# Two gate tiles moved beside the rotation, the other gates and the latent turns put in one sequence, the combination placed earlier

## What is computed

```python
qkv_a = proj[..., :IN_A]
q_c = proj[..., IN_A:IN_A + B_Q_RANK]
kv_c = proj[..., IN_A + B_Q_RANK:IN_A + B_Q_RANK + B_KV_RANK]
gates = jax.nn.sigmoid(proj[..., IN_A + IN_B:] + b_gate)
g_a, g_b = gates[..., :D_MODEL], gates[..., D_MODEL:]
o_a = mixer_dilated(qkv_a, pos) @ w_o_a
o_b = mixer_mla(q_c, kv_c, k_pe, pos, mla_q_norm, mla_w_uq, mla_kv_norm, mla_w_ukv) @ w_o_b
mix = (g_a * o_a + g_b * o_b) @ w_out
```

## Time and profile before

| | us |
|---|---|
| median of three runs (lowest, highest) | 1642.92 (1642.27, 1648.21) |
| the profiled execution, its own time | 1641.97 |
| its span, first to last instruction | 1640.2 |
| TensorE busy | 1531.1 |
| first rotation and turns | 170.2 to 184.7 |
| first attention, its first score to its last instruction | 185.4 to 340.2 |
| stage with the combination, TensorE's first product to VectorE's last instruction | 340.5 to 378.1 |

### The profile page before, as it was taken

The page is one execution under the profiler, slowest core; times in us unless marked ns, Lnnn a source line. Parts: engine busy times, 40 slices in busy tenths (PEclk is TensorE's granted clock), DMA queues, the critical chain, the costliest instruction groups (busy, mean ns, idle before and its releaser), DMA issues. The chain is left out here.

```text
span 1640.2 us, 18642 instructions
## 1 busy us (share of the span) xinstructions
PE 1531.1 (93%) x7560; PEld 1241.9 (76%) x7560; DVE 809.4 (49%) x1166; ACT 575.8 (35%) x902; POOL 282.6 (17%) x296
## 2 busy tenths in 40 slices
PE   7989699787999999999998999988799999999997
PEld 5878588685677888888886766766678888888885
DVE  4232433357756545434346786377755444324425
ACT  4221533435744433223235322285324222112212
POOL 0000000000032599000003265413222000000000
PEclk9999899789999999999999989989689999999998
DMA  4322121130022323322232212110012233222322
GB/s 174 103 78 80 52 78 46 45 104 26 2 85 93 105 92 103 103 90 90 103 128 62 77 53 77 58 52 27 1 52 77 78 103 103 102 80 100 103 90 77
DMA packets 38858, 129.25 MB, mean 79 GB/s; under 512 B 4676, under 2 KB 23004, under 8 KB 27380
## 3 DMA queue, kind: packets, MB, share of 16 engines
q1 hardware_dynamic: 38484, 127.93, 22.7%
q10 hardware_dynamic: 288, 0.12, 0.0%
HBM read 124.82 MB, written 3.17 MB: 78 GB/s over the span
## 5 line engine op out<-in xcount | busy, mean ns | idle before, releaser
L223 DVE TENSOR_TENSOR ring_lo<-ring_raw,ring_hi 128x2048 fp32r<-128x2048 f32 (+3 forms) x115 | 265.8, 2314 | 203.5 <-ACT ring_hi L213 203.4
L242 PE MATMUL bank<-xT_hi,ring_hi 128*128 128x512 f32 (+3 forms) x920 | 356.2, 387 | 5.9 <-DVE xT_lo L1570 4.7
L242 PE MATMUL bank<-xT_lo,ring_hi 128*128 128x512 f32 (+3 forms) x920 | 352.7, 383 | 0.0
L242 PE MATMUL bank<-xT_hi,ring_lo 128*128 128x512 f32 (+3 forms) x920 | 352.5, 383 | 0.0
L213 ACT CAST ring_hi<-ring_raw 128x2048 fp32r<-128x2048 f32 (+3 forms) x115 | 212.8, 1852 | 241.9 <-DMA ring_raw<-in_w_ff 131.1
L242 PEld LDWEIGHTS bank<-xT_hi,ring_hi 128*128 128x128 f32 (+2 forms) x920 | 174.1, 189 | 47.4 <-issue 7.6
L242 PEld LDWEIGHTS bank<-xT_hi,ring_lo 128*128 128x128 f32 (+2 forms) x920 | 174.0, 189 | 34.3
L242 PEld LDWEIGHTS bank<-xT_lo,ring_hi 128*128 128x128 f32 (+2 forms) x920 | 174.2, 189 | 33.1
L242 PE MATMUL bank<-ring_hi,hid_hi 128*128 128x512 f32 x432 | 169.6, 393 | 3.8 <-DVE ring_lo L223 3.8
L242 PE MATMUL bank<-ring_hi,hid_lo 128*128 128x512 f32 x432 | 169.1, 391 | 0.0
L242 PE MATMUL bank<-ring_lo,hid_hi 128*128 128x512 f32 x432 | 169.0, 391 | 0.0
(11 more groups left out here) (496 smaller groups left out, 2157.8 us busy)
## 6 DMA issues: line engine op xcount, KB each, us to landing
ring_raw<-in_w_ff SPq DMA_DIRECT2D x30, 1024.0 KB, 4.9
ring_raw<-in_w_up SPq DMA_DIRECT2D x22, 1024.0 KB, 4.9
ring_raw<-in_w_proj SPq DMA_DIRECT2D x8, 1024.0 KB, 5.2
ring_raw<-in_w_gates SPq DMA_DIRECT2D x8, 1024.0 KB, 4.9
ring_raw<-in_w_fm SPq DMA_DIRECT2D x12, 512.0 KB, 4.7
ring_raw<-in_w_dn_a SPq DMA_DIRECT2D x6, 1024.0 KB, 4.8
ring_raw<-in_w_proj SPq DMA_DIRECT2D x8, 512.0 KB, 4.5
ring_raw<-in_w_out SPq DMA_DIRECT2D x4, 1024.0 KB, 4.9
```

What stands on the lines that cost most here:

```text
L223: k.nc.vector.tensor_tensor(k.ring.lo[:, g % SLOTS, 0:n], k.raw[:, g % SLOTS, 0:n], plain(k.ring.hi[:, g % SLOTS, 0:n]), ALU.subtract).the ...
L242: mm = k.nc.tensor.matmul(out, x, y, start=first and n == 0, stop=last and n == 3 * len(pairs) - 1)
```

## The change

- `GatesAndTurns` no longer spreads halves evenly. It is given one sequence of tiles (`order`) that share the banks 6 and 7 by their place in it: gates 0 to 12, turn 0, gate 13, turn 1, gate 14, turn 2, gate 15, turns 3, 4, 5. A tile waits until the one two places ahead is released: a gate when kept, a turn when its low part is made.
- Gates 0 and 1 are made at the head of TensorE's stream in the first turn stage, ahead of its wait for the rotation. ScalarE keeps gate 0 between the squares and the scaling of the latents, gate 1 behind the scaling. SP issues chunk 16 there, behind its wait for gate 1.
- The rounds are written out: gates 2 to 12 (22 halves) over rounds 0 to 19, then turns and gates 13 to 15 mixed in rounds 20 to 24, turns 4 and 5 in round 26, behind the last mixes.
- At round 0 ScalarE and VectorE split chunk 15, which gate 1's end no longer asks for.
- In the combination the weights move from tile 7 to 5, exponential from 8 to 6, sums and first addition from 9 to 6, the other additions from 10 and 11 to 7 and 8, the rotation of the queries from 13 to 10.

```diff
-class GatesAndTurns(Beside):
+class GatesAndTurns:
...
+        self.place = {x: n for n, x in enumerate(order)}
+
+    def bank(self, x):
+        return self.k.pb[6 + self.place[x] % 2]
+
+    def released(self, x):
+        kind, n = x
+        return (self.free.sem, self.free.base + n + 1) if kind == "gate" else (self.low.sem, self.low.base + n + 1)
...
+    def sync_begun(self, sp):
+
+        issue_chunks(self.k, sp, self.first + 1 + SLOTS)
...
+    def unit(self, pe, kind, n, half):
+        k, x = self.k, (kind, n)
+        if half == 0 and self.place[x] >= 2:
+
+            pe.wait_ge(*self.released(self.order[self.place[x] - 2]))
+        if kind == "turn":
...
+        g, _, _, pairs, _, _ = self.steps[n]
+        wait_chunk(k, pe, g)
+        w = len(pairs) // 2
+        mm = products(k, self.bank(x)[:, :], pairs[half * w:half * w + w], half == 0, half == 1)
+        if half:
+            mm.then_inc(self.done.sem, 1)
...
+    def act(self, act, r):
         k = self.k
...
+        if r == 0:
+            split_hi(k, act, self.first + 1 + LEAD)
+        for kind, n, half in self.rounds.get(r - 1, ()):
+            if kind == "turn":
+                _, f, dst, gain = self.turns[n]
+                act.wait_ge(self.turned.sem, self.turned.base + n + 1)
+                k.nc.scalar.mul(dst.hi[:, f, :], self.bank((kind, n))[:, :], gain).then_inc(self.high.sem, 1)
+            elif half:
+                self.keep_gate(act, n)
+                if n % 2:
+                    split_hi(k, act, min(self.steps[n][0] + 1 + LEAD, self.end + LEAD))
...
@@ -908,6 +949,8 @@
                 if i < nb:
                     turn(i)
                     turn(i + 1)
+            for r in range(nb + 2, beside.steps_on_pe) if paired else ():
+                beside.pe(pe, r)
...
-            if paired and beside.steps_on_pe > nb:
-                beside.act(act, nb + 1)
+            for r in range(nb + 1, beside.steps_on_pe + 1) if paired else ():
+                beside.act(act, r)
...
             if norms is not None:
-                norms.act(act)
+                norms.squares(act)
+                gates.keep_gate(act, 0)
+                norms.scale(act)
+                gates.keep_gate(act, 1)
...
         @block.tensor
         def _(pe):
+            for n in range(2) if gates is not None else ():
+                for half in range(2):
+                    gates.unit(pe, "gate", n, half)
             if before is not None:
...
+    order = [("gate", n) for n in range(13)] + [("turn", 0), ("gate", 13), ("turn", 1), ("gate", 14), ("turn", 2),
+                                                ("gate", 15), ("turn", 3), ("turn", 4), ("turn", 5)]
+    units = [("gate", n, half) for n in range(2, 13) for half in range(2)]
+    rounds = {r: units[len(units) * r // 20:len(units) * (r + 1) // 20] for r in range(20)}
+    rounds.update({20: [("turn", 0, 0), ("gate", 13, 0)], 21: [("gate", 13, 1), ("turn", 1, 0)],
+                   22: [("gate", 14, 0), ("gate", 14, 1)], 23: [("turn", 2, 0), ("gate", 15, 0)],
+                   24: [("gate", 15, 1), ("turn", 3, 0)], 26: [("turn", 4, 0), ("turn", 5, 0)]})
+    beside = GatesAndTurns(k, steps, evac_gates, turns, order, rounds)
     norms = LatentNorms(k, qc, kvc, 195)
-    stage_turn(k, items, rope_a, norms=norms)
+    stage_turn(k, items, rope_a, sync=beside.sync_begun, norms=norms, gates=beside)
...
     def act(self, act, j):
-        if j == 8:
+        if j == 6:
...
-        elif j == 7:
+        elif j == 5:
             self.weights(dve)
-        elif j == 9:
+        elif j == 6:
             self.sums(dve)
             self.add(dve, 0)
-        elif j in (10, 11):
-            self.add(dve, j - 9)
-        elif j == 13:
+        elif j in (7, 8):
+            self.add(dve, j - 6)
+        elif j == 10:
             self.rope_query(dve)
```

More of the change, by code:

```diff
@@ L727, in __init__, with squares @@
         self.sq, self.mean, self.root, self.scaled = (k.sig("norm_" + n) for n in ("sumsq", "mean", "root", "scaled"))
-    def act(self, act):
+    def squares(self, act):
+        n = 0
         a = self.k.nc.scalar
-        n = 0
         for src, width, ms, _ in self.parts:
@@ L738, in act, with scale @@
                 n += 1
+    def scale(self, act):
+        a = self.k.nc.scalar
         for i, (src, width, _, rs) in enumerate(self.parts):
@@ L757, in close, with __init__, sync, pool @@
         self.scaled.base += 2 * T
-class GatesAndTurns(Beside):
[L765 to L768, removed]
-        self.turned, self.high, self.low = (k.sig("norm_" + n) for n in ("turned", "evac_act", "evac_dve"))
+class GatesAndTurns:
+    def __init__(self, k, steps, evac, turns, order, rounds):
+        self.k, self.steps, self.evac, self.turns, self.order, self.rounds = k, steps, evac, turns, order, rounds
+        self.steps_on_pe = max(rounds) + 1
+        self.done, self.free = k.sig("beside_done"), k.sig("beside_free")
+        self.turned, self.high, self.low = (k.sig("norm_" + n) for n in ("turned", "evac_act", "evac_dve"))
+        note_freed(k, steps, self.done)
+        self.first, self.end = steps[0][0], steps[-1][0] + 1
+        self.place = {x: n for n, x in enumerate(order)}
[4 more added lines that the diff above has]
+        return (self.free.sem, self.free.base + n + 1) if kind == "gate" else (self.low.sem, self.low.base + n + 1)
+    def sync(self, sp):
+        issue_chunks(self.k, sp, self.end + SLOTS)
+    def sync_begun(self, sp):
+        issue_chunks(self.k, sp, self.first + 1 + SLOTS)
+    def pool(self, pool):
+        pass
+    def unit(self, pe, kind, n, half):
[3 more added lines that the diff above has]
+        if kind == "turn":
+            src, f, _, _ = self.turns[n]
+            for t in range(T):
+                mm = k.nc.tensor.transpose(self.bank(x)[:, t * P:(t + 1) * P], src[:, t, f * P:(f + 1) * P], k.ident[:, :])
+            mm.then_inc(self.turned.sem, 1)
+            return
+        g, _, _, pairs, _, _ = self.steps[n]
[4 more added lines that the diff above has]
+            mm.then_inc(self.done.sem, 1)
+    def keep_gate(self, act, n):
+        act.wait_ge(self.done.sem, self.done.base + n + 1)
+        self.evac(act, n, self.bank(("gate", n))[:, :]).then_inc(self.free.sem, 1)
@@ L771, in pe @@
     def pe(self, pe, r):
+        for u in self.rounds.get(r, ()):
+            self.unit(pe, *u)
+    def act(self, act, r):
         k = self.k
[L773 to L797, removed]
@@ L799, in dve @@
-    def dve(self, dve, r):
[L800 to L807, removed]
+        if r == 0:
+            split_hi(k, act, self.first + 1 + LEAD)
@@ new lines, in dve @@
+    def dve(self, dve, r):
+        k = self.k
+        if r == 0:
+            split_lo(k, dve, self.first + 1 + LEAD)
+        for kind, n, half in self.rounds.get(r - 1, ()):
+            if kind == "turn":
+                _, f, dst, gain = self.turns[n]
+                dve.wait_ge(self.high.sem, self.high.base + n + 1)
+                k.nc.vector.scalar_tensor_tensor(out=dst.lo[:, f, :], in0=self.bank((kind, n))[:, :], scalar=gain,
+                                                 in1=plain(dst.hi[:, f, :]), op0=ALU.mult,
+                                                 op1=ALU.subtract).then_inc(self.low.sem, 1)
+            elif half and n % 2:
+                split_lo(k, dve, min(self.steps[n][0] + 1 + LEAD, self.end + LEAD))
@@ L809, in close @@
     def close(self):
-        super().close()
+        self.done.base += len(self.steps)
+        self.free.base += len(self.steps)
         for s in (self.turned, self.high, self.low):
@@ L1014, in _ @@
                     evac("dve", dve, i + 1)
-            if paired and beside.steps_on_pe > nb:
-                beside.dve(dve, nb + 1)
+            for r in range(nb + 1, beside.steps_on_pe + 1) if paired else ():
+                beside.dve(dve, r)
             for i in range(nb + 2) if not paired else ():
@@ L1178, in turned_as, with stage_turn @@
     return bank[0:m, :].rearrange("p (a c) -> p c a", c=form) if form else bank[0:m, :]
-def stage_turn(k, items, before=None, sync=None, norms=None):
+def stage_turn(k, items, before=None, sync=None, norms=None, gates=None):
     nc = k.nc
@@ L1729, in rope_a, with evac_gates @@
         return x
+    steps, j = [], 0
+    for _ in range(8):
+        s, j, g = gemm(k, g, KD, 8, feature_tiles(k.xT, (0, P), 2 * P), j, banks=(6, 7))
+        steps += s
+    def evac_gates(act, j, ps):
+        return nc.scalar.activation(gates[:, j, :], ps, ACT.Identity, bias=col(k, "b_gate", j))
+    qcT = k.split("qcT", 104, [P, 4, S], 112)
+    kvcT = k.split("kvcT", 128, [P, 2, S], 132)
+    turns = [(qc, f, qcT, col(k, "q_norm", f)) for f in range(4)] + [(kvc, f, kvcT, col(k, "kv_norm", f)) for f in range(2)]
+    order = [("gate", n) for n in range(13)] + [("turn", 0), ("gate", 13), ("turn", 1), ("gate", 14), ("turn", 2),
[6 more added lines that the diff above has]
```

(4 more changed lines are left out.)

## The result

| | before | changed |
|---|---|---|
| median of six runs (lowest, highest) | 1642.64 (1641.86, 1648.21) | 1631.12 (1624.21, 1633.38) |
| profiled execution, own time | 1641.97 | 1624.21 |
| its span | 1640.2 | 1622.4 |

The ratio is 0.9927, with a 95% interval of 0.9906 to 0.9948: 11.5 us less, where the forecast's sum was 11.3 less (1631.5 with a range of 1627.5 to 1637.5). The profiled execution of the changed kernel happens to be the lowest of its six; which part of its distance from the median belongs to the change is settled by a second profile further down.

A forecast was written before the change was run, and what follows sets the result against it. TensorE, busy 93% of the span, was taken as the bound, with only its waiting or low-clock time winnable. Terms +4.2 - 27.5 + 0.3 + 11.1 + 3.4 - 2.8 = -11.3 us gave 1631.5 us, range 1627.5 to 1637.5.

The forecast's parts named there:

- Step 1: First turn stage: two gate tiles beside the rotation delay the first score from 185.4 to 189.6, +4.2 us.
- All hidden but 0.3 us: ScalarE in the first turn stage: keeping gates 0 and 1 delays copies only 0.3 us, absorbed by four banks.
- Step 2: Rounds 0 to 19, first attention: ten fewer half tiles, -27.5 us, and a +0.3 us wait, if TensorE stays the bound.
- the wait for gate 8: Round 11: gate 8 needs gate 6 kept, which ScalarE does after that pair's exponentials, +0.3 us.
- Rival (c): Rounds 0 to 19: a pair's chain exceeding 8.3 us bounds; at 11.08 us per pair, 1659 us; chance 0.04.
- Step 3: Rounds 20 to 26: added gates and their order cost +11.1 us, plus +3.4 us of clock.
- The waits: Late first attention: TensorE stalls for kept gates, gate 13 until T+4.6, gate 14 for 4.6 us from T+15.8.
- T: End of the scores of rounds 20 and 21, first attention; 306.29 us before, forecast near 283.
- The clock behind the two: After the two late stalls: half clock loses 1.7 us each, +3.4 us, bounds 0 and 11.
- Rival (a): Late first attention: the stalls cost the clock for long, 5 us each instead of 1.7, 1638 us; chance 0.15.
- Step 4: Turn stage behind the attention: the earlier combination ends VectorE's work at 375.3 instead of 378.05, -2.8 us.

The follow-up runs named there:

- second profile: The changed kernel run once more, nothing altered, for another profile and more times: median 1632.16 us (kernel before 1643.25), ratio 0.9934.
- the one with only two gates: Against the kernel before: gates 0 and 1 beside the rotation, the other 28 halves over rounds 0 to 19, old combination; 1636.67 us, ratio 0.9954.

## Why the prediction was right, point by point

**Step 1 (+4.2) was right in its sum and half wrong in its reasons.** Measured +4.4 with the clock back 4.5 us after the start. "All hidden but 0.3 us" holds for the changed kernel only because the second tile stands in front: with one tile the place of the scaling on ScalarE costs 3.54 us of waiting on TensorE. I had checked when ScalarE is free against when the first turn is due, with two tiles in the queue, and took the result for a property of the order. The remark that a tile in the idle time is a gain and one behind it is none was borne out within the noise, once the scaling stood first (5.9 against 6.3 us).

**Step 2 (-27.2) was right**, to 0.3 us. TensorE stayed the bound, the pairs shrank by the gate halves taken out, and the 0.3 us are the wait for gate 8 that did not come. Rival (c), the chain of a pair, never came near: TensorE did not idle in the ten pairs.

**Step 3 (+14.5 with the clock) was right, mis-sized inside.** The sequence alone brings nothing that can be measured, as its working said by costing it at +11.1 and +3.4 against 16.5 of moved gates. The waits were placed and sized from the order of ScalarE's work alone: one until 4.6 us behind T, where the row has 289.57 - 284.96 = 4.61, and one of 4.6, where the row has 4.45. The clock behind the two was put at 3.4 us; the kernels that take the waits away show 2.7 to 4.6. Rival (a) would have needed 10. The reason that the forecast gave for its low value, that 512-column products follow both waits, is not shown: the stretches at half clock behind the waits were 3.1 and 2.9 us in the first profile, 2.9 and 6.3 in the second and 6.0 and 4.5 with the sequence alone, with the same products behind them. That the first profile came so close to 1.7 us for each is in part luck. The term varies from run to run with the clock: T to the next stage took 48.3 us in the first profile, 333.42 - 283.50 = 49.9 in the second, and 50.9 in the kernel with the sequence alone, with the same work in it.

**Step 4 (-2.8) was right in direction and too small.** 3.9 us less in the changed kernel, 2.9 in the profile of the part alone, 4.7 in its median. Of the 1.1 us about half is the exponential: I let its table load begin when the weights are done. It began at 346.15, when ScalarE's copy had ended and before the weights' first instruction at 346.24, so that the exponential was ready before tile 5's copy ended and the sums followed that copy without a gap. From the weights to the sums it took 348.20 - 346.24 = 1.96 us, where the forecast has 2.5. Another 0.3 us is a slip in the sum: the list of work that is full before lasts 378.05 - 359.35 = 18.7 us and lasts 366.90 - 348.20 = 18.7 us now, so from 356.3 it ends at 375.0 and not at 375.3. The last 0.3 us lies ahead of the weights, which start 13.0 us into the stage instead of the 13.3 us assumed. The Trainium skill (ScalarE: Activation LUTs, "Table sets: the hidden batching unit") gives about 2.7 us for a load, and one load for a logarithm followed by an exponential. The traces decide otherwise: every load in them took 1.28 us, and one was there although a logarithm had been computed before it.

**The rest.** The forecast of the median came out 0.4 us off. Part of that is luck: the errors of the four steps have both signs (+0.2, -0.3, -0.4, -1.1 in the first profile, sum 1.6 too high), and in the second profile the same stretches came 0.7 us longer than forecast.

## What to carry to other kernels

When work is moved into an idle stretch, ask which other engine's order the move changes: the keeping of a result placed ahead of work that used to run in that stretch can cost more than the work gained, and a second piece of filler may only hide it. A buffer that is freed behind another chain's work on an in-order engine is a wait of that chain's length; moving three half tiles to an earlier round took away two such waits and was worth about as much as the whole change (13.1 us against 11.5). And cost a wait of TensorE at its length plus the slow stretch behind it, with a range: that stretch varied here from one execution to the next.

## What the runs showed of the hardware

- The activation table load ran while its activation still waited for its data: it started at 346.15 with the weights' first instruction at 346.24, at 347.06 with them at 347.15 in the second profile, and at 353.98 with them at 354.08 in the kernel with the combination alone. In these three the load was hidden in ScalarE's idle time.
- The same code behind the attention took 1255.2, 1261.8 and 1266.1 us in three profiles. That is 10.9 us, 0.7% of the whole, so single executions of this kernel can't be compared below that, whatever their first 380 us show.
- Around T, behind each wait of 4 to 4.8 us the clock fell to 1.2 GHz, and how long it stayed there was not fixed even for the same code. Where 512-column gate products followed, full clock was back 2.9 to 6.3 us after the wait (seven waits in four profiles). Where mixes, scores and turns followed, it was back after 6.2 to 8.1 us in ten of twelve waits; in the other two, one each in the kernel before and in the one with only two gates, it was not back when the next wait began. No run here varies the kind of work alone.
